# Three expert visits of 64 slots with the high and low halves as one stationary matrix, in a hybrid decoder trunk on one core

## The reference, cut to what matters

```python
logits = hf @ w_router                        # 256 x 8
topv, topi = lax.top_k(logits, 2)
wts = softmax(topv)
gate = sum(one_hot(topi, 8) * wts[..., None], axis=1)
for e in range(8):
    out = out + gate[:, e:e+1] * ((silu(hf @ wg[e]) * (hf @ wu[e])) @ wd[e])
```

## Time and profile before

| | us |
|---|---|
| median of 3 runs | 1738.53 (1737.38 to 1738.98) |
| the profiled execution, its device time | 1738.88 |
| its span | 1736.9 |
| of it before the first visit | about 730 |
| eight visits, start to start | 124.0 each |
| busy: PE / DVE / ACT / POOL over the span | 1713.0 / 1278.9 / 1057.8 / 23.8 |

### The profile page before, as it was taken

One profiled execution on the slowest core, in us unless ns is written; L12 is line 12 of the kernel. 1 busy time (PEld: TensorE's weight loads), 2 busy tenths in 40 slices (PEclk: granted clock), 3 DMA queues, 4 the chain that ended last, 5 costly groups with the idle time before them and its releaser, 6 DMA issues. The chain is left out here.

```text
span 1736.9 us, 24368 instructions
## 1 busy us (share of the span) xinstructions
PE 1713.0 (99%) x9681; PEld 1500.5 (86%) x9681; DVE 1278.9 (74%) x935; ACT 1057.8 (61%) x852; POOL 23.8 (1%) x56
## 2 busy tenths in 40 slices
PE   8999999999999999899999999999999999999997
PEld 8999889989899989788888888888888888888886
DVE  5555655454565564698898898888888888988986
ACT  5443555343454454477777777777777776777774
POOL 1000000000000010100000000000000000000000
PEclk9999999999999999999999999999999999999999
DMA  9555634464665553799899899899899899898970
GB/s 323 186 179 170 218 128 157 153 218 164 207 194 179 183 185 122 291 328 366 342 366 371 330 363 373 337 362 375 334 358 381 329 351 372 337 362 330 381 270 25
DMA packets 164064, 477.54 MB, mean 275 GB/s; under 512 B 8516, under 2 KB 13732, under 8 KB 164004
## 3 DMA queue, kind: packets, MB, share of 16 engines
q1 hardware_dynamic: 164004, 476.69, 76.0%
HBM read 475.61 MB, written 1.05 MB: 274 GB/s over the span
## 5 line engine op out<-in xcount | busy, mean ns | idle before, releaser
L470 ACT ACTIVATE whi<-raw 128x2048 fp32r<-128x2048 f32 (+1 forms) x260 | 493.1, 1897 | 268.9 <-PE ps L1196 108.1
L1468 PE MATMUL ps<-whi,a_hi 128*128 128x512 f32 x1792 | 558.5, 393 | 0.0
L795 DVE TENSOR_TENSOR wlo<-raw_more,whi 128x2048 fp32r<-128x2048 f32 x192 | 438.6, 2292 | 63.6 <-ACT whi L470 63.3
L470 ACT ACTIVATE whi<-raw_more 128x2048 fp32r<-128x2048 f32 x192 | 367.2, 1917 | 78.6 <-PE ps L1497 44.7
L790 DVE TENSOR_TENSOR wlo<-raw,whi 128x2048 fp32r<-128x2048 f32 (+1 forms) x116 | 259.0, 2236 | 210.9 <-ACT whi L470 210.8
L1468 PEld LDWEIGHTS ps<-whi,a_hi 128*128 128x128 f32 x1792 | 332.2, 188 | 69.2 <-DVE wlo L795 2.3
L795 DVE TENSOR_TENSOR wlo<-raw,whi 128x2048 fp32r<-128x2048 f32 x144 | 327.0, 2289 | 59.3 <-ACT whi L470 59.3
L1468 PE MATMUL ps<-wlo,a_hi 128*128 128x512 f32 x896 | 349.8, 390 | 0.0
L1196 PE MATMUL ps<-a_hi,whi 128*128 128x256 f32 x992 | 281.4, 284 | 0.0
L1196 PE MATMUL ps<-a_hi,wlo 128*128 128x256 f32 x992 | 280.7, 283 | 0.0
L1196 PE MATMUL ps<-a_lo,whi 128*128 128x256 f32 x992 | 280.7, 283 | 0.0
(11 more groups left out here) (208 smaller groups left out, 1681.6 us busy)
## 6 DMA issues: line engine op xcount, KB each, us to landing
raw_more<-in_w_e_up SPq DMA_DIRECT2D x80, 1024.0 KB, 6.9
raw_more<-in_w_e_gate SPq DMA_DIRECT2D x64, 1024.0 KB, 6.7
raw<-in_w_e_down SPq DMA_DIRECT2D x64, 1024.0 KB, 6.8
raw<-in_w_e_gate SPq DMA_DIRECT2D x48, 1024.0 KB, 7.2
raw_more<-in_w_e_down SPq DMA_DIRECT2D x48, 1024.0 KB, 7.2
raw<-in_w_in SPq DMA_DIRECT2D x32, 1024.0 KB, 5.2
raw<-in_w_e_up SPq DMA_DIRECT2D x32, 1024.0 KB, 7.1
raw<-in_w_xk SPq DMA_DIRECT2D x8, 1024.0 KB, 5.2
```

The costliest lines, as they stand in the source:

```text
L470: return act.activation(dst, src, ACT.Copy, scale=scale)
L795: return dve.tensor_tensor(dst, src, hi.bitcast(F32), ALU.subtract)
L1468: ins = pe.matmul(bank(b0 + c), (heh, hel)[xi][:, kt, :], w[wi][:, k, c * C:(c + 1) * C], start=kt == 0 and n == 0, stop=kt == KD - 1 and ...
```

## The change

Three of the eight visits are "light": the experts with the fewest tokens, expert 7 left out. Expert 7 is the first visit, the three light ones are the second to fourth, and the others follow by load. A light visit has 64 slots instead of 128. S holds each slot twice (columns 0 to 63 and 64 to 127), and ACT and DVE put the high half of the activations in stationary columns 0 to 63 and the low half in 64 to 127. A weight block then takes two matmuls (by high weights, by low weights) instead of three, and the two halves of the output stand in different PSUM partitions. For the gate and up sums they are added when the block is transposed: ACT copies both sums out of PSUM, and PE multiplies each block by `fold2`, two 64-column identities on top of each other, in plain float32. Silu, product and split then run on the transposed, folded blocks of 128 x 4 x 64. For the down sum the scatter adds the halves, since both carry the same slot. The three loops are written out for visits 0 to 5 and run as a loop only for the last ones. POOL works out the order of experts, the tables of ranks and gates by visit, and the number of visits (16 if a light expert has over 64 tokens or another over 128); SP reads the expert's number for each visit from it.

```diff
+HP = P // 2
+FIRST = 7
+RANK_OF_VISIT = (7, 0, 1, 2, 3, 4, 5, 6)
+LIGHT = (1, 2, 3)
+STEADY = 6
...
+        LIGHT_T_AFTER = {**T_AFTER, NJ - 1: DOWN[-1] - 3}
... SP
-                    load_expert_unit(i, 0)
-                with sp.Fori(0, NE - 1) as e:
-                    load_rest(e, e)
-                    load_first(e + 1, e + 1)
-                load_rest(NE - 1, NE - 1)
+                    load_expert_unit(i, FIRST)
+                load_rest(FIRST, 0)
+                sp.wait_ge(s["eid_ready"], 1)
+                for v in range(1, NE):
+                    e = sp.value_load(eid[0:1, v:v + 1], min_val=0, max_val=NE - 1)
+                    load_first(e, v)
+                    load_rest(e, v)
... POOL, after h_tok
+                pool.wait_ge(s["hg_ready"], NT)
+                link(pool.tensor_tensor(fold2[:], ident[:, 0:HP], ident[:, HP:P], ALU.add))
+                pool.wait_ge(s["count_ready"], 1)
...
+                compare(less, key, key, ALU.is_lt)
+                total(by_load[:], less)
+                compare(at_visit, by_load, rank_of, ALU.is_equal)
+                per_visit(eidf[:], e_iota[:])
+                pool.tensor_copy(eid[:], eidf[:]).then_inc(s["eid_ready"], 1)
...
+                ins.then_inc(s["table_ready"], 1)
...
+                ins.then_inc(s["gatev_ready"], 1)
...
+                                   ).then_inc(s["visits_ready"], 1)
... ACT
+                def light_visit(v):
+                    for i in range(AHEAD, BODY):
+                        expert_hi(i, v)
+                        if i == AHEAD:
+                            y_hi(v)
+                        for g, (j, n) in enumerate(GROUPS):
+                            if i == GATE[g] + 2 * n + 1:
+                                act.wait_ge(s["unit_used"], v * BODY + (U0 + GATE[g] + 2 * n))
+                                if g == 0:
+                                    act.wait_ge(s["act_ready"], v * NJ)
+                                else:
+                                    act.wait_ge(s["t_done"], v * NJ + j)
+                                for c in range(n):
+                                    copy(silu_t[c][:], bank(c)).then_inc(s["gs_ready"], 1)
+                            if i == UP[g] + 2 * n + 1:
+                                act.wait_ge(s["unit_used"], v * BODY + (U0 + UP[g] + 2 * n))
+                                act.wait_ge(s["t_done"], v * NJ + j)
+                                for c in range(n):
+                                    copy(act_t[c][:], bank(2 + c)).then_inc(s["us_ready"], 1)
+                        for j in range(NJ):
+                            if i == LIGHT_T_AFTER[j] + 2:
+                                act.wait_ge(s["t_done"], v * NJ + (j + 1))
+                                act.activation(st[:], bank(6)[:, 0:4 * HP].rearrange("p (f c) -> p f c", c=HP), ACT.Silu
+                                               ).then_inc(s["silu_ready"], 1)
+                            if i == LIGHT_T_AFTER[j] + 3:
+                                act.wait_ge(s["act_ready"], v * NJ + (j + 1))
+                                copy(aTh[j % 2][:, :, 0:HP], at_[:]).then_inc(s["acthi_ready"], 1)
+                    next_visit(v, HP if v + 1 in LIGHT else P)
... DVE, light_visit
+                            if i == LIGHT_T_AFTER[j] + 2:
+                                dve.wait_ge(s["silu_ready"], v * NJ + (j + 1))
+                                dve.wait_ge(s["actT_ready"], v * NJ + j)
+                                dve.tensor_tensor(at_[:], st[:], bank(6)[:, 4 * HP:].rearrange("p (f c) -> p f c", c=HP),
+                                                  ALU.mult).then_inc(s["act_ready"], 1)
+                            if i == LIGHT_T_AFTER[j] + 3:
+                                dve.wait_ge(s["acthi_ready"], v * NJ + (j + 1))
+                                minus(aTh[j % 2][:, :, HP:], at_[:], aTh[j % 2][:, :, 0:HP]).then_inc(s["actT_ready"], 1)
... DVE, ahead of the first visit
-                link(dve.tensor_tensor(rt[2][:, 0, :], rt[1][:, 0, :], rt[1][:, 1, :], ALU.add))
-                link(dve.tensor_reduce(cnt[:, 0:1], rt[2][:, 0, :], AX_X, ALU.max))
-                link(dve.tensor_scalar(cnt[:, 1:2], cnt[:, 0:1], float(P), float(NE), ALU.is_gt, ALU.mult))
... PE
+                def light_gate_up(i, v):
+                    w_name, g, part = order[i]
+                    n_c = GROUPS[g][1]
+                    kk, b0 = 4 // n_c, 0 if w_name == "gate" else 2
+                    if part == 0 and g:
+                        pe.wait_ge(s["gs_ready" if w_name == "gate" else "us_ready"],
+                                   LIGHT.index(v) * NJ + GROUPS[g][0])
...
+                        for c in range(n_c):
+                            for n in range(2):
+                                ins = pe.matmul(bank(b0 + c), heh[:, kt, :], w[n][:, k, c * C:(c + 1) * C],
+                                                start=kt == 0 and n == 0, stop=kt == KD - 1 and n == 1)
+                def light_fold(j, v):
+                    pe.wait_ge(s["us_ready"], LIGHT.index(v) * NJ + (j + 1))
+                    if j == 0:
+                        pe.wait_ge(s["xadd_done"], v * 4 + 1)
+                    else:
+                        pe.wait_ge(s["act_ready"], v * NJ + j)
+                    for h, src in enumerate((silu_t, act_t)):
+                        for f in range(4):
+                            ins = pe.matmul(bank(6)[:, (4 * h + f) * HP:(4 * h + f + 1) * HP],
+                                            src[j % 2][:, f * P:(f + 1) * P], fold2[:], start=True, stop=True)
+                    ins.then_inc(s["t_done"], 1)
...
-                pe.wait_ge(s["visits_ready"], 1)
-                visits = pe.value_load(nvis[0:1, 0:1], min_val=NE, max_val=2 * NE)
-                with pe.Fori(0, visits) as v:
+                for v in range(STEADY):
+                    visit(v, v in LIGHT)
+                pe.wait_ge(s["visits_ready"], 1)
+                visits = pe.value_load(nvis[0:1, 0:1], min_val=NE, max_val=2 * NE)
+                with pe.Fori(STEADY, visits) as v:
+                    visit(v)
```

More of the change, by code:

```diff
@@ new lines, in _ @@
+                ins.then_inc(s["table_ready"], 1)
+                pool.wait_ge(s["gate_ready"], 1)
+                for t in range(NT):
+                    per_visit(gatev[:, t, 0:NE], gate[:, t, :])
+                    ins = pool.tensor_copy(gatev[:, t, NE:2 * NE], gate[:, t, :])
+                ins.then_inc(s["gatev_ready"], 1)
+                link(pool.tensor_tensor(over[:], count[:], cap[:], ALU.subtract))
+                link(pool.tensor_scalar(over[:], over[:], 0.0, None, ALU.is_gt))
@@ L731, in silu, with y_hi @@
                         act.wait_ge(s["act_ready"], v * NJ + (j - 1))
+                    elif not (isinstance(v, int) and v == 0):
+                        act.wait_ge(s["t_done"], v * NJ)
                     act.activation(silu_t[j % 2][:], bank(j % 2), ACT.Silu).then_inc(s["silu_ready"], 1)
-                def visit(v, more):
+                def y_hi(v):
+                    act.wait_ge(s["unit_used"], v * BODY + U0)
+                    copy(yh, ps[:, 4:6, :].rearrange("p a b -> p (a b)"), gc[:, 0:1]).then_inc(s["yhi_ready"], 1)
@@ new lines, in next_visit @@
+                def next_visit(v, slots):
+                    expert_hi(BODY, v)
+                    gathered_hi(v + 1, slots)
+                    for i in range(1, AHEAD):
+                        expert_hi(BODY + i, v)
+                def light_visit(v):
[26 more added lines that the diff above has]
+                    next_visit(v, HP if v + 1 in LIGHT else P)
@@ L736, in visit @@
+                def visit(v, more, slots=P):
                     act.activation(first_silu[:], mhalf[:, 0:1], ACT.Silu)
@@ L752, in visit @@
                     if more:
[L753 to L756, removed]
+                        next_visit(v, slots)
                 expert_hi(AHEAD - 1, 0)
@@ L1117, in visit @@
                                 act_lo(j, v)
[L1118 to L1125, removed]
+                        scattered(i, v, slots)
@@ L1157, in _ @@
                 for t in range(NT):
[L1158 to L1161, removed]
+                    ins = dve.scalar_tensor_tensor(out=gate[:, t, :], in0=rt[0][:, t, :], scalar=rc[5][:, t:t + 1],
+                                                   in1=rt[5][:, t, :], op0=ALU.mult, op1=ALU.add)
+                ins.then_inc(s["gate_ready"], 1)
+                for v in range(STEADY):
+                    if v in LIGHT:
+                        light_visit(v)
+                    else:
+                        visit(v, True, HP if v + 1 in LIGHT else P)
                 dve.wait_ge(s["visits_ready"], 1)
                 last_visit = dve.value_load(nvis[0:1, 1:2], min_val=NE - 1, max_val=2 * NE - 1)
-                with dve.Fori(0, last_visit) as v:
+                with dve.Fori(STEADY, last_visit) as v:
```

(15 more changed lines are left out.)

166 lines of the change are left out of this document (127 added, 39 removed).

## The result

The changed kernel takes **1714.2 us** (median of 4 runs, 1712.8 to 1715.8) against 1738.0 in four runs of the kernel before beside it; the ratio is 0.9863, with a 95% interval of 0.9846 to 0.9880. That is 24 us less; the prediction was 1712, 27 less.

What follows compares the result with a forecast made beforehand. PE bounds the 124.0 us visits; in three light ones DVE's 103.0 plus 9.5 and 2.6 of losses makes 115, saving 9 each, 27 in all: 1738.9 - 27 gives 1712 us, range 1695 to 1728.

Steps and rivals of the forecast that it cites:

- What bounds a heavy visit: Visits of 128 slots: bound by PE, 124.0 us each, its parts summing to 123.7; five of eight stay at 124.0.
- PE's work in a light visit: Light visit: PE's sum 95.2 us, from matmuls 76.3, seven folds 12.6 (1.8 each), gather 3.6, scatter 1.8, transposes of S 0.9.
- DVE as the next bound: Light visit: DVE's work sums to 103.0 us, 92.4 of it low parts; next engine to bind, but with gaps.
- the ring: Light visit: low part, PE's unit, high part and handovers take 6.4 us for three units, leaving inserts 0.2 us of slack.
- the 9.5 + 2.6 for groups and visit's end: Light visit: DVE loses 9.5 us over 3.5 groups of two chunks, and 2.6 to the uncovered gather at the end.
- the hand-worked one: Light visit: one group of two chunks, 12 units, followed start by start; it loses 2.7 us.
- one of the things by which I had said I would be wrong: Light visits: wrong if PE waits for something other than the low part, such as a PSUM copy or a product.
- Rival A: Light visits: PE's clock falls when PE idles; at the lower clock 60% of a visit, 152 us and 1823 in all; 5%.
- Transfers: Light visits: 44.04 MB in 115 us ask for 383 GB/s; loaded units lie ready for about 30 us; nothing is charged.
- Rival B: Light visits: transfers end last if the rate is 375 GB/s at best; 117.4 to 121 us a visit, 1719 to 1730; 12%.
- The ring's cause: Light visit: three buffers of split weights tie ACT, DVE and PE into a ring with hardly any slack.
- POOL's chain: Ahead of the visits: 38 linked instructions to gatev_ready take 11 to 27 us, ready by 755, hidden before PE asks at 777.4.

Runs made afterwards that it cites:

- experiment 2: The changed kernel with no light visits (LIGHT = ()), unrolled loops and POOL's tables kept: 1738.1 us, ratio 0.9999 against the kernel before.
- experiment 6: On top of experiment 1, DVE makes the low part of only half the columns of each unit in light visits: 1667.9 us.
- experiment 1: The changed kernel with ACT's copies of the last chunk's sums waiting for the fold two chunks back, one count lower: 1701.7 us, ratio 0.9791.
- experiment 3: The changed kernel with light visits loading only half the columns of each unit, same number of transfers: 1713.6 us, ratio 0.9862.
- experiment 9: On top of experiment 1, five light visits instead of three, number of visits fixed at 8, tokens beyond the 64th left out: 1676.6 us.
- experiment 11: The changed kernel with experiment 1's relaxed wait, six pairs of split buffers, seven raw buffers and the fold in fp32r: 1686.2 us.
- experiment 5: On top of experiment 1, every fold done twice: 1739.0 us.
- experiment 8: On top of experiment 1, the fold in fp32r instead of plain float32: 1686.5 us, ratio 0.9703.
- experiment 4: The changed kernel with six pairs of split buffers instead of three, seven raw buffers instead of fourteen: 1709.0 us; with experiment 1's relaxed wait too: 1696.6 us.
- experiment 7: On top of experiment 1, silu, product and split of chunks 2 to 5 one unit later, folds of chunks 3 and 5 in PSUM bank 7: 1702.7 us.

## Why the prediction was right

**What bounds a heavy visit: right.** Visits of 128 slots stayed at 124.0, also written out (experiment 2).

**PE's work in a light visit: nearly right.** A fold takes 1.71 us (940.92 to 942.63 in the first light visit) where I took 1.8 from instructions of 8 to 128 columns. In experiment 6 PE is busy for 97.0 with four waits for a low part; a busy time counts the 0.16 us by which a last matmul outlasts its share, so the sum is above 96, not 95.2. One part of it: the first matmul behind a fold stands 0.31 us from the next (942.63 to 942.94), not 0.227.

**DVE as the next bound, with the ring right behind: right.** Its sum, 103.0, was measured as 103.6 (ACT's, 89.7, as 90.9). The length of 115 was met by 115.0, with 11.4 of waits for 12.1 predicted. But the parts of it differ: 3.2 of the 11.4 is the needless wait (experiment 1), so the ring's own losses are 8.2. The term mis-sized is the 9.5 + 2.6 for groups and visit's end: it was 3.9 too high for what it stood for, and left out the 3.2 of the last group, which I had copied from the hand-worked one though its single chunk makes the count one too high. Which group, or the end, I charged too much was not measured. That the two errors nearly cancel was luck. PE's longest wait is released by DVE's low part, as forecast, but what stands behind it is a copy out of PSUM, one of the things by which I had said I would be wrong.

**Size.** 27 us forecast, 24.9 in the profiled execution's visits. The missing 2.2 is the clock in the second light visit, which I had said would stay at 1.00. Rival A was right in its mechanism and wrong in its size: 2.2 us in one visit, not tens, because after the gap PE is busy and the clock comes back:

```profile
1075.00:1080.00 5.00, 5.00 (x32) 4.41 (x31) 2.75 (x3) 2.92 (x4) 0.00 (x0) 1.00 1.00 366
```

The Trainium skill ("TensorE: Matmul & The Clock Gate", Part 1) says that activity releases the clock; the rows agree, with 0.61 granted in 1070 to 1076 us, where PE is busy throughout, and 1.00 from 1075.

**Transfers: right that they were not the bound.** Rival B is refuted by experiments 3 and 9: half the bytes bring nothing, and the rate was not 375 at best but 394 over four distances in a row and 407 over one. Transfers hold ACT only in faster variants (experiment 11 and, for 3.0 us, the third light visit of experiment 6). The Trainium skill ("DMA: Bandwidth & Descriptors", Where 436 GB/s comes from) says that for transfers from HBM the HBM side binds, at about 358 GB/s a core; the same page, under Measured, calls that the share with both cores of the memory streaming. Taken as a limit for a core alone it would have spoken for rival B: as an estimate from that page's figure, 44.04 MB would take 123 us. With one core at work the measured 407 GB/s lies above it, which agrees with the second statement.

**The ring's cause: half right.** I put the lack of slack down to three split buffers. Inserts do pass through one to one (experiments 1, 5 and 8), and the shorter folds of experiment 8 halve the losses (107.0 against DVE's 103.0). But six buffers close only 1.1 of 8.2 us (experiment 4). The written order, in which ACT waits for PE between two high parts, may tie them as well; of what is left I have not shown which wait is worth what, and experiment 7 took the wrong one.

**POOL's chain:** gates were ready at 746 us, inside the 738 to 755 forecast, and PE asked at 778.

## What to carry to other kernels

When the work of the binding engine is cut and the sums of three engines then lie within 15% of each other (here 103.0, 95.2 and 89.7), sum each of them, and then ask for the slack of the loop that ties them: here 6.4 us for three units against 6.6, so that what was added to a fold or taken from it came through in full, with no engine full. Not every wait is worth its length: one that counted one too many cost all of its 3.3 us, and the longest single waits in the list led to it, while cutting ACT's waits for folds from 9.9 us to 3.6 gained nothing in experiment 7, where a new wait of PE came up. A gap on PE can cost twice, once itself and once in clock.

## What was not expected of the hardware

- A plain float32 matmul with 64 moving columns costs nearly as much as one with 128: 16 instructions, two a matmul, in 1.71 us (0.107 each) against 0.112 in the gather. In fp32r it is one instruction, and a fold takes 1.00 us.
- The same gap of 3.4 us on PE brought the lower clock in the second light visit of the changed kernel and not in the first or third; in experiment 3, and in experiment 4 with six buffers and the gap, all three had it. It cost 2.2 us where the matmuls stood 0.43 apart for 6 us, and 1.0 where they did so for 3.4 us (experiment 3). In experiment 7 a gap of 1.9 us was enough. So a time can spread by about 2 us a gap without any change of the work.
- POOL's instructions took 0.2 to 0.4 us, but some of the same form 2.3 us when they started just behind one of DVE's low parts:

```profile
735.57 0.32 POOL L516 TENSOR_TENSOR table<-table,rank 128x64 f32<-128x64 f32 x1
...
736.92 2.30 DVE L921 TENSOR_TENSOR wlo<-raw,whi 128x2048 fp32r<-128x2048 f32 x1 [2.02 <-ACT whi L553]
737.03 2.37 POOL L516 TENSOR_TENSOR table<-table,gate 128x64 f32<-128x64 f32 x1
```

It is the reverse of the earlier trace rows, where DVE was held up by POOL. Nothing here waited for it.
